# A hybrid encoder block: rankings moved apart from the block fronts, score buffer, squares on ScalarE

## The reference

```
h = RMSNorm(x);  q,k,v,xc,B,C = h @ W_in               # six parts of 512
sb = StickBreaking(QKNorm(q), QKNorm(k), v)            # 8 heads x 64, strictly causal
cv = B * causal_depthwise_conv3(C * xc)
x  = x + concat(RMSNorm(sb), RMSNorm(cv)) @ W_out
h2 = RMSNorm(x);  q1,q2 = halves of h2 @ W_q           # 8 heads x (128+128)
v1,i1 = top16(q1 @ keys0.T);  v2,i2 = top16(q2 @ keys1.T)
top, pos = top16 of the 256 sums v1[i]+v2[j];  idx = i1*128 + i2;  g = softmax(top)
y  = x + sum over 8 heads x 16 picks of g * gelu(u[idx] . h2) * v[idx]
```

## Time and profile before

| | |
|---|---|
| median of 3 runs | 3099.83 us (3098.99 to 3100.64) |
| the profiled execution | 3104.61 us, span of its trace 3102.7 us |
| busy, share of the span | PE 73%, DVE 66%, ACT 34%, POOL 38% |
| granted TensorE clock, mean | 0.848 of 2.4 GHz |
| DMA | 1210.54 MB, mean 390 GB/s over the span |

### The profile page before, as it was taken

The page is one execution under the profiler, slowest core; times in us unless marked ns, Lnnn a source line. Parts: engine busy times, 40 slices in busy tenths (PEclk is TensorE's granted clock), DMA queues, the critical chain, the costliest instruction groups (busy, mean ns, idle before and its releaser), DMA issues. The chain is left out here.

```text
span 3102.7 us, 28744 instructions
## 1 busy us (share of the span) xinstructions
PE 2275.9 (73%) x8992; PEld 1038.4 (33%) x8992; DVE 2057.3 (66%) x4906; ACT 1067.8 (34%) x3119; POOL 1180.7 (38%) x1037
## 2 busy tenths in 40 slices
PE   7787678887886659887886656987887665555555
PEld 5543333543342213633342312443444221111111
DVE  2577785557688885467687786557868888544444
ACT  1233332245233332266332332247623333222222
POOL 0133233334334443244433443334433444444443
PEclk9898878988988769889988878999998887777777
DMA  6799999989999999999999999999998999999998
GB/s 205 265 398 378 393 419 371 389 365 380 394 366 421 421 419 371 399 385 417 419 379 382 421 421 372 392 381 422 402 416 330 422 420 421 421 422 420 418 422 347
DMA packets 184903, 1210.54 MB, mean 390 GB/s; under 512 B 20656, under 2 KB 20784, under 8 KB 53680
## 3 DMA queue, kind: packets, MB, share of 16 engines
q0 software_dynamic: 147456, 1073.81, 84.2%
q1 hardware_dynamic: 37296, 134.91, 11.4%
HBM read 1204.44 MB, written 4.19 MB: 390 GB/s over the span
## 5 line engine op out<-in xcount | busy, mean ns | idle before, releaser
L441 POOL DMA_INDIRECT ring<-table_uv,idx_t x1024 | 1178.8, 1151 | 1897.9 <-PE acc L624 1583.3
L1020 DVE CUSTOM_DVE_ANT_0 ring<-ring,h2r 128x1024 f32<-128x1024 f32 x1024 | 1244.9, 1224 | 814.5 <-DMA ring<-table_uv,idx_t 809.6
L624 PE MATMUL acc<-ring,wmask 128*64 128x512 f32 x4096 | 1246.7, 742 | 520.2 <-ACT wmask L754 505.3
L624 PEld LDWEIGHTS acc<-ring,wmask 128*64 128x64 f32 x4096 | 297.6, 160 | 1274.8 <-ACT wmask L754 781.2
L750 ACT ACTIVATE acts<-dots 128x2 f32<-128x2 f32 x512 | 103.7, 203 | 1501.9 <-DVE dots L1020 1501.2
L754 ACT ACTIVATE wmask<-gmask,acts 128x64 f32<-128x64 f32 x1024 | 300.6, 340 | 49.0 <-ACT acts L750 1.5
L743 ACT ACTIVATE gmask<-stack,gate_t 128x64 f32<-128x64 f32 x1024 | 293.0, 334 | 0.1
L461 PE MATMUL pt<-hT,w_ring 128*128 128x256 f32 (+1 forms) x1440 | 277.0, 349 | 4.0 <-DVE uT L936 3.5
L461 PEld LDWEIGHTS pt<-hT,w_ring 128*128 128x128 f32 x1440 | 234.6, 197 | 64.4 <-issue 41.9
L461 PE MATMUL po<-hT,w_ring 128*128 128x256 f32 (+1 forms) x800 | 167.0, 366 | 22.7 <-ACT kT L675 14.2
L461 PEld LDWEIGHTS po<-hT,w_ring 128*128 128x128 f32 x800 | 138.2, 208 | 66.5 <-issue 52.2
(11 more groups left out here) (158 smaller groups left out, 1776.3 us busy)
## 6 DMA issues: line engine op xcount, KB each, us to landing
w_ring<-wstream SPq DMA_DIRECT2D x240, 512.0 KB, 7.9
ring<-table_uv,idx_t POOLq DMA_INDIRECT x1024, 12.2
xs<-x_in_dram SPq DMA_DIRECT2D x8, 512.0 KB, 10.3
y_out_dram<-xs SPq DMA_DIRECT2D x8, 512.0 KB, 8.1
g_all<-norm SPq DMA_DIRECT2D x1, 512.0 KB, 7.1
keysT<-keys SPq DMA_DIRECT2D x1, 128.0 KB, 6.4
chan_sb<-chan SPq DMA_DIRECT2D x1, 19.0 KB, 6.6
```

What stands on the lines that cost most here:

```text
L441: nc.gpsimd.indirect_dma_start(out=ring[:, t % SLOTS, :], out_offset=None, in_=table, in_offset=bass.IndirectOffsetOnAxis(ap=idx_t[:, b % ...
L624: mm = nc.tensor.matmul(acc[HALF * i:HALF * i + HALF, half * 512:(half + 1) * 512], wmask[:, slot, :], ring[:, slot, D + half * 512:D + (h ...
L1020: d = V.tensor_tensor_reduce(u, u, h2r[:, b % H_SLOTS, i, :], 1.0, 0.0, ALU.mult, ALU.add, dots[:, t % SLOTS:t % SLOTS + 1])
```

## The change

- **Rankings apart.** `front_steps` holds no rankings (other than the very first); `timetable` adds ranking r = 4b + q on its own: eleven steps at ticks 32r - 36 + RANK_TIME, that is from 36 to 10 ticks ahead of the first gather that uses it (the first ones are squeezed after tick -1). So one ranking runs in every 32 ticks up to tick 982.
- **Score buffer.** The scaled scores of a quarter go to one of 7 slots of `scores` and stay there until ranked; match_replace works in place, and `pairs` (1024 wide) holds the 256-sums and the one-hot rows. `idx_t` and `gate_t` shrink to one block. `look_up` works on 1024-wide operands where it had two of 512.
- **Fronts spread.** WHEN is now `(-1, -1, 6), (8, 74, 96), (92, 216, 262), (264, 450, 500), (518, 705, 755)`: main part, then the key queries of quarters 1 to 3. `pause` entries leave ticks free after norm, roots and adds.
- **Both blocks side by side.** Squares of x and of the second norm are ScalarE activations with accumulated output; one inverse root serves both blocks (also for q/k, 32 sums, and for the output norms); copies and transposes of the two blocks use `rb`/`rc` and `pt`/`pz`; convolution channel groups alternate between two pairs of banks for two-block fronts, so that the waits of PE for `u_ready` and `cv_ready` go back one group further.
- **Slots.** X_SLOTS 4, H_SLOTS 2, gmask 4 slots. SP loads x of blocks 1 to 3 at piece 32 of front 0, and of block b + 4 right behind the store of block b, for which it waits. `h2` of blocks 3, 5 and 7 moves to ticks 262, 518 and 774.

```diff
-WHEN = [(-1, 2, 20, 42, 62), (0, 70, 80, 90, 100), (100, 236, 266, 298, 328), (328, 488, 520, 552, 584),
-        (584, 744, 776, 808, 840)]
+WHEN = [(-1, -1, 6), (8, 74, 96), (92, 216, 262), (264, 450, 500), (518, 705, 755)]
+RANK_TIME = [0, 2, 4, 7, 9, 11, 14, 15, 17, 20, 26]
+RANK_LEAD = 36
+H2_AT = {3: 262, 5: 518, 7: 774}
...
+    for r in range(1, BLOCKS * QUARTERS):
+        b, q = divmod(r, QUARTERS)
+        for (_, step), k in zip(rank_steps(b, q), RANK_TIME):
+            start = QPICKS * r - RANK_LEAD
+            tick = start + k if start >= 0 else -1 + k * (QPICKS * r - 10) // RANK_TIME[-1]
+            out.setdefault(tick, []).append((super_of(b), *step))
...
+def score_slot(b, q):
+    return 3 + q if b % 2 else q % 3
...
+        def conv_banks(n, c):
+            return (po[:], bank_a, bank_b) if n == 2 and c % 2 else (po[:], bank_c, bank_d)
...
                     if k == finish_tick(b):
                         store(b)
+                        if b + X_SLOTS < BLOCKS:
+                            load_x(b + X_SLOTS)
...
-                    wait(pe, (xc_kept, u_ready, cv_ready)[i], 4 * f + c)
+                    if n == 1:
+                        wait(pe, (xc_kept, u_ready, cv_ready)[i], 4 * f + c)
+                    elif i == 0:
+                        wait(pe, xc_kept, 4 * f + c)
+                    elif c > 1:
+                        pe.wait_ge((u_ready, cv_ready)[i - 1], 4 * f + c - 1)
...
+                if name == "norm":
+                    act.wait_ge(x_in[b % 2], 16 * (b // 2 + 1))
+                    nc.scalar.activation((rc, rb)[i][:], xs[:, b % X_SLOTS, :], ACT.Square,
+                                         accum_out=ss1[:, i:i + 1]).then_inc(x_squared, 1)
...
+                        wait(act, s_ranked, score_slot_before(b0 + t, q))
+                        nc.scalar.activation(scores[:, score_slot(b0 + t, q), :], (bank_a, bank_b)[t], copy,
                                              scale=invh[:, t:t + 1]).then_inc(s_ready, 1)
+                if name == "h2_square":
+                    act.wait_ge(added, 4 * b0 + 4 * n)
+                    nc.scalar.activation((rc, rb)[i][:], xs[:, b % X_SLOTS, :], ACT.Square,
+                                         accum_out=ssh[:, i:i + 1]).then_inc(h2_squared, 1)
...
+                    settle()
                     for c in mine:
-                        last = V.match_replace(left(c), top_v[:, c, 0:8], here(c), TAKEN)
+                        step(V.match_replace(here(c), top_v[:, c, 0:8], here(c), TAKEN))
...
-                    for t in range(n):
-                        dve.wait_ge(x_in[(b0 + t) % 2], 16 * ((b0 + t) // 2 + 1))
-                        square_sum(xs[:, (b0 + t) % X_SLOTS, :], rc[:], ss1[:, t:t + 1])
-                    settle()
+                if name == "root1":
+                    dve.wait_ge(x_squared, b0 + n)
                     inverse_root(inv1[:, 0:n], ss1[:, 0:n], n, 1.0 / D, done=norm1)
...
+                    if b:
+                        dve.wait_ge(gmask_ready, ((b - 1) * PICKS + (q + 1) * QPICKS) // 2)
```

More of the change, by code:

```diff
@@ L80, in front_steps, with w, pause @@
     piece = 2.2 * n
[L81 to L89, removed]
+    def w(*pieces):
+        return [(piece, ("w", j)) for j in pieces]
+    def pause(ticks):
+        return 0.0, ("pause", ticks)
+    main = [(1.0, ("norm", b)) for b in blocks] + [pause(2), (6.0, ("root1", blocks[0])), pause(6)]
+    main += [(3.0, ("h", b)) for b in blocks] + [(3.0, ("hT", b)) for b in blocks] + [pause(3)]
+    main += w(*range(PIECE_V)) + [(1.0, ("qk_square", b)) for b in blocks] + w(8)
+    main += [(6.0, ("qk_root", blocks[0]))] + w(9, 10) + [(3.0, ("qk_scale", b)) for b in blocks] + w(11) + [pause(2)]
+    main += [(3.0, ("qk_turn", b)) for b in blocks]
     conv = []
     for c in range(CH):
-        conv += [(piece, ("w", PIECE_CONV + 3 * c + i)) for i in range(3)] + [(2.0 * n, ("conv", c))]
+        conv += w(*range(PIECE_CONV + 3 * c, PIECE_CONV + 3 * c + 3)) + [(2.0 * n, ("conv", c))]
     turns = [(b, p) for b in blocks for p in range(passes(b))]
@@ L137, in front_steps @@
-    main += peer(0)
-    sections = [main, [], [], []]
-    for q, section in enumerate(sections):
-        mine = [step for b in blocks for step in ranks(b, q)]
-        ahead = [(0.6, step) for _, step in peer(q + 1)] if q < 3 else []
-        last_rank = max(k for k, (_, step) in enumerate(mine) if step[0] == "rank")
-        for k, step in enumerate(mine):
-            section.append(step)
-            while len(ahead) > 1 and k >= last_rank * (5 - len(ahead)) // 5:
-                section.append(ahead.pop(0))
-            if k == last_rank:
-                section += ahead
-                ahead = []
@@ L150, in front_steps @@
-    return sections
+    main += [pause(4)] + [(4.0, ("x_turn", b)) for b in blocks] + [(1.0, ("h2_square", b)) for b in blocks]
+    main += [pause(3), (4.0, ("h2_root", blocks[0])), (2.0, ("h2", blocks[0]))]
+    main += w(*range(PIECE_PEER, PIECE_PEER + 4)) + [(3.0, ("key_scores", 0))]
+    if f == 0:
+        first, early = rank_steps(0, 0), 2 if n == 1 else 1
+        main += first[:6]
+        rest = []
+        for q in range(1, 4):
+            (main if q <= early else rest).extend(
+                w(*range(PIECE_PEER + 4 * q, PIECE_PEER + 4 * q + 4)) + [(3.0, ("key_scores", q))])
+        return main + first[6:], rest
@@ L861, in combine @@
                     step(V.max_index(sum_p[:, c, 0:8], best(c, 0), here(c)))
-                    step(V.match_replace(left(c), best(c, 0), here(c), TAKEN))
+                    settle()
+                    step(V.match_replace(here(c), best(c, 0), here(c), TAKEN))
                     return
```

290 lines of the change are left out of this document (138 added, 152 removed).

## The result

The changed kernel takes 3045.16 us at the median of four runs (3040.90 to 3050.72); the kernel before took 3100.23 beside it (3098.99 to 3105.31). The ratio is 0.982 (95% interval 0.980 to 0.984), a gain of 55 us where 53 had been predicted. Sign and size were right. The sum was right in part because errors of opposite sign cancelled, and what follows is mostly about those. A few microseconds in one stage may be such chance.

A forecast was written before the change was run, and what follows sets the result against it. The kernel was taken as bound by DMA transfers, with 228 us lost to local chains delaying mixes. Terms -19 + 1 - 12 + 12 - 34 - 3 + 2.4 = -52.6 us off 3099.83 gave 3047 us, 8-in-10 range 3000 to 3095.

The forecast's parts named there:

- What bounds the kernel: Whole kernel: bound by DMA transfers, with 228 us lost where local chains hold back mixes; DVE load alone costs nothing at 86%.
- Ends: Ends of the three two-block fronts: rankings no longer follow one another, gain 34 us of 44.5, bounds 20 and 40.
- rival 2: Stalls at the ends are PE's, not the rankings'; half the gain, 3076 us; chance 0.14.
- Attention: Three attention stages: rankings now run inside and fill DVE, cost 12 us (6, 2, 4), bounds 0 and 76.
- Rival 1: Attention stages: rankings make DVE the bound, 77 us above the 12 taken, 3124 us; chance 0.10.
- Projections and convolution: Two-block fronts up to first scores: second banks and mostly longer stages gain 12 us of 41.8, bounds 0 and 25.
- Starts: Starts of the three two-block fronts: ScalarE squares, spaced root, side-by-side copies gain 19 us of 25.3, bounds 8 and 23.
- waits 3.37 us for x: Start of the last front: ScalarE stands 6.3 us for block 7's x; cost 1 us, bounds 0 and 7.
- Start-up: Before the first gather: ScalarE squares first, so its copy comes 3.6 us later; cost 2.4 us, bounds 0 and 6.
- rival 3: Convolution pieces: spreading PE's work leaves more of the fronts at 1.2 GHz, 3111 us; chance 0.05.
- Rivals 4 and 5: 4: starts, ends, projections lose nothing, 3004 us, chance 0.09; 5: a slot-order wait in each quarter, 3105 us, chance 0.05.

The follow-up runs named there:

- first experiment: The kernel before, with first-quarter rankings of two-block fronts given 2.5 times their schedule length and section borders 8 to 20 ticks later: 3054.95 us, ratio 0.9862.
- second: The changed kernel, with each ranking's eleven steps packed into 8 ticks where they had 26: 3088.38 us, ratio 0.9959 to the kernel before.

## Why the prediction was right, point by point

**What bounds the kernel: right.** The same bytes, 64 us less loss, and DVE's total nearly unchanged. Wider spacing at the ends brought 46 us to the kernel before (first experiment), and packing the rankings took 43 to 52 of the change's 55 to 65 away (second).

**Ends: right, too small.** 42 us, not 34. I left 3 to 4 us each for what would be late next; nothing is, at 0.5 to 1.0 us. As a time rival 2 is out, 3076 us. Its mechanism, that these stalls are PE's, is not. Rows of the kernel before, at the end of the front of blocks 4 and 5:

```profile
1584.57 1.94 PE L624 MATMUL acc<-ring,wmask 128*64 128x512 f32 x8
...
1586.44 3.72 PE L461 MATMUL po<-hT,w_ring 128*128 128x256 f32 x16
...
1590.54 1.94 PE L624 MATMUL acc<-ring,wmask 128*64 128x512 f32 x8
...
1593.87 0.49 DVE L826 MAX8 top_v<-rb 128x8 f32<-128x128 f32 x2 [7.42 <-ACT rb L725]
...
1637.91 0.65 PE L604 MATMUL small<-turn_src,ident 128*64 128x32 f32 x8 [9.13 <-DVE turn_src L905]
```

At first PE runs without a wait, with a key piece and key scores between two mixes, and the mixes are 5.97 us apart where two ticks of transfers take 4.98; DVE waits 7.42 us for the key scores before its first ranking step. Some 40 us later it is the other way round: PE waits 9.13 us for the ranking. The change spreads both, the key pieces and the rankings, and so does the first experiment. The second packs the rankings alone, and the ends lose only some 7 us more by it. How the 42 us divide between the two is not shown; a run with the key pieces packed and the rankings spaced would show it.

**Attention: the load was right, what it costs was not.** I had worked out 207 us less 15 of slack, which is 192 us of DVE work in ticks 585 to 669; the trace has 192.27. From that I booked +12 us for three stages. With the stage at 221.5 us, DVE was 87% loaded, and behind the first 30 us nothing was lost in the front of blocks 4 and 5 (421 GB/s) and 5.1 us in the last. By my own test, over 90% and 405 to 418 GB/s in ticks 585 to 668, both missed: the row has 87% and 401, the rate being low because of the passage in its first 30 us. Rival 1's mechanism is real, as the added reductions show, but what it cost was measured at loads that the change doesn't reach: 90 to 93% over a stretch. Its bound of 76 us came from the ends of the kernel before, with DVE at 83 to 84%; but the earlier trace rows has 86% at 421 GB/s, so the load alone was not the price there. A price taken from a stretch with another local order is the term of the sum that failed.

**Projections and convolution: a third of what I took.** 4 us for 12. The second pair of banks, which I had credited, gives nothing in sum. And I had seen the passage to attention as column sums and scores lying between two mixes, a matter of their length. The length is unchanged (3.58 us); the wait before it grew from 5.35 to 10.11 and POOL's from 13.15 to 15.11. Two free ticks on either side of the sums remove that wait, and the time falls by 15 to 23 us, 13 of them at the passages in the trace. It was the largest term left, and I had not named it as a wait of PE on DVE.

**Starts: 10.7 for 19.** The test I had set, no wait of POOL above 8 us, failed in all three: POOL waits 10.19 us at 479.83, 9.71 at 998.60 and 11.42 at 1718.78. The last front's start after:

```profile
1686.05 1.04 ACT L688 ACTIVATE rc<-xs 128x1024 f32<-128x1024 f32 x1
1686.99 0.19 ACT L688 ACTIVATION_READ_ACCUMULATOR rc<-xs 128x1 f32 x1
1690.54 1.06 ACT L688 ACTIVATE rb<-xs 128x1024 f32<-128x1024 f32 x1 [3.37 <-DMA xs<-x_in_dram]
...
1712.78 1.13 ACT L692 ACTIVATE rb<-xs,inv 128x1024 f32<-128x1024 f32 x1
1713.97 1.97 PE L482 MATMUL pt<-ident,rb 128*128 128x128 f32 x8 [9.07 <-ACT rb L692]
...
1718.78 1.40 POOL L473 DMA_INDIRECT ring<-table_uv,idx_t  x1 [11.42 <-PE acc L660]
```

ScalarE waits 3.37 us for x, where I had 6.3, and that is covered. What is late is the transpose: PE waits 9.07 us for the copy, with the next mix queued behind it, as it did before for the root. The wait in order had moved, not gone; a quarter left was too little, and over half was.

**Start-up: the shift was right, the time partly luck.** The copy moved from 9.99 to 13.84 us, 3.85 where 3.6 was worked out, and the first gather went out at 136.30, inside the 133 to 137 that I had given. The loss grew by 3.4 us. But the same steps give anything from 129.74 to 137.29, and over 76:125 the granted clock was 0.83 in this execution and 0.93 in that of the kernel before. So part of the 3.4 us is the clock's and not the copy's.

**Clock: rival 3 is out.** The convolution stages stand at a granted clock of 0.92 to 0.95, before at 0.89 to 0.92. The two passages are lower, at 0.67 and 0.69. At the first the sums run at the lower level with the stall (3.58 us) and without it (3.58), and the rate over 1120:1200 is 361 and 413 GB/s, so there the clock is not what costs. The Trainium skill ("TensorE: Matmul & The Clock Gate", section "What's actually happening") holds that activity releases the throttle; the trace agrees at the first passage, where the lower clock stands right behind PE's wait of 10.11 us. Where the clock did cost is a place that no rival named, the front before the first gather.

**Rivals 4 and 5.** More went at the ends, not elsewhere, so 3004 was not met; what it lacks is at the passage and the starts. A wait in the slot order does not show: the long ranking stretch runs at 419 GB/s. (Rival 5's own figures, 32 x 2 us on 3047, make 3111 us, not 3105.)

## What to carry to other kernels

Where one engine executes a fixed order and a buffer ahead of it is a few us deep, side work costs by how much of it stands between two steps of the main loop, not by its share of the engine: a DVE busy for 83 to 86% stood beside 421 GB/s in a ranking stretch and beside 337 to 353 at the ends, and packing each ranking into 8 ticks cost 43 to 52 us without adding work. A rate for a new placement must come from a stretch with that placement; a total load began to count here between 84 and 90%. And wherever one engine's queue holds a step that another engine's in-order step must precede, leave main-loop steps between the two: here two ticks on either side were worth 15 to 23 us, while new banks, moved squares and later waits gave nothing that could be measured.

## What the runs showed of the hardware beyond that

- A square with accumulated output on ScalarE is two instructions, ACTIVATE 1.04 us and ACTIVATION_READ_ACCUMULATOR 0.19, together about DVE's 1.22 us.
- Sixteen column sums of one column each take 3.58 us at the lower granted clock (0.50 over 1158.2:1161.7 in the run with room around them) and 1.95 at full clock (1867.24, the same run).
- DVE can be 84% busy beside gathers at 412 to 421 GB/s; at 93% they fall to 373.
- The time to the first gather varied by 7.6 us between eight profiled kernels of one start-up order, and follows the clock granted over 76:125, from 1.00 to 0.83. A difference of a few microseconds between single executions can be this alone.
